# Trunk step on one core: squares of the output norm added on VectorE, one batch of token sums, and modulation steps in other places

## What is computed

```python
mod = silu(c) @ w_ada + b_ada              # nine rows of 1024: shift, scale, gate for three sublayers
x = x + 0.5 * gt1 * swiglu(rmsnorm(x) * (1 + sc1) + sh1)
proj = (rmsnorm(x) * (1 + scm) + shm) @ w_in
v = silu(layernorm(depthwise_causal_conv(a * sigmoid(g))) )     # 512 channels
p = pool_mix(u_pool)                                            # 512 channels
x = x + gtm * (concat[v, p] @ w_out)
x = x + 0.5 * gt2 * swiglu(rmsnorm(x) * (1 + sc2) + sh2)
y = rmsnorm(x)
```

## Time and profile before

| | |
|---|---|
| median of three runs | 1001.75 us |
| lowest, highest run | 1000.78, 1003.18 us |
| span of the profiled execution | 1000.3 us |
| mean granted TensorE clock in it | 0.995 of full speed |
| busy: TensorE, VectorE, ScalarE, GpSimd | 99%, 68%, 54%, 61% |
| TensorE idle while waiting, the longest after the start | 0.7, 0.6, 0.5 us |

### The profile page before, as it was taken

The page is one execution under the profiler, slowest core; times in us unless marked ns, Lnnn a source line. Parts: engine busy times, 40 slices in busy tenths (PEclk is TensorE's granted clock), DMA queues, the critical chain, the costliest instruction groups (busy, mean ns, idle before and its releaser), DMA issues.

```text
span 1000.3 us, 20132 instructions
## 1 busy us (share of the span) xinstructions
PE 986.4 (99%) x7589; PEld 948.4 (95%) x7589; DVE 676.6 (68%) x1391; ACT 538.4 (54%) x1000; POOL 610.6 (61%) x529
## 2 busy tenths in 40 slices
PE   9999999999999999999999999999999999999997
PEld 8899999999999998889977898999999999999996
DVE  3787766676666644469996447976666676666676
ACT  5756554566554542373264436665545665555664
POOL 3267666677676563346877143577666676766673
PEclk9999999999999999999999999999999999999998
DMA  9922322232224327745214622223222222223222
GB/s 360 376 82 90 123 85 86 86 117 94 85 86 168 128 85 291 271 160 204 85 34 169 254 91 79 85 85 118 93 86 86 102 111 85 86 90 122 85 86 95
DMA packets 22717, 127.52 MB, mean 127 GB/s; under 512 B 4192, under 2 KB 7392, under 8 KB 8032
## 3 DMA queue, kind: packets, MB, share of 16 engines
q1 hardware_dynamic: 19744, 105.28, 29.1%
q10 hardware_dynamic: 2880, 20.97, 5.5%
HBM read 123.06 MB, written 3.19 MB: 126 GB/s over the span
## 4 chain that ended last, share of the span: by engine, by line
PE 94%; POOL 2%; DVE 1%; ACT 1%; issue 1%; DMA 0%; DVEq 0%; POOLq 0%; ACTq 0%
PE tile_a L777 23%; PE tile_b L777 23%; PE ada_ps L777 18%; PE tile_a L610 8%; PE tile_b L610 7%; PE tile_a L750 3%; PE ada_ps L582 2%; PE tile_b L750 2%; PE tile_a L944 1%; PE tile_b L632 1%; POOL last_taps L2479 1%; PE ada_ps L956 1%; PE stat_ps L874 1%; PE tile_a L1019 1%; PE tile_a L661 1%
## 5 line engine op out<-in xcount | busy, mean ns | idle before, releaser
L2327 POOL TENSOR_TENSOR w_lo<-w_raw,w_hi 128x512 fp32r<-128x512 f32 (+1 forms) x177 | 226.0, 1283 | 96.1 <-ACT w_hi L1134 95.6
L2327 POOL TENSOR_TENSOR w_lo<-s_raw,w_hi 128x512 fp32r<-128x512 f32 (+1 forms) x118 | 152.3, 1292 | 74.5 <-ACT w_hi L1134 74.5
L1134 ACT ACTIVATE w_hi<-w_raw 128x512 fp32r<-128x512 f32 (+1 forms) x177 | 109.4, 619 | 66.8 <-PE ada_ps L777 53.4
L777 PE MATMUL tile_a<-x_hi,w_hi 128*128 128x288 f32 x400 | 118.7, 297 | 0.0
L777 PE MATMUL tile_b<-x_hi,w_hi 128*128 128x288 f32 x400 | 118.5, 296 | 0.0
L777 PE MATMUL tile_b<-x_lo,w_hi 128*128 128x288 f32 x400 | 118.2, 295 | 0.0
L777 PE MATMUL tile_a<-x_lo,w_hi 128*128 128x288 f32 x400 | 118.2, 295 | 0.0
L777 PE MATMUL tile_a<-x_hi,w_lo 128*128 128x288 f32 x400 | 117.8, 295 | 0.0
L777 PE MATMUL tile_b<-x_hi,w_lo 128*128 128x288 f32 x400 | 117.8, 294 | 0.0
L2283 POOL TENSOR_TENSOR w_lo<-w_raw,w_hi 128x2048 fp32r<-128x2048 f32 x13 | 59.7, 4591 | 80.6 <-ACT w_hi L1109 77.6
L777 PE MATMUL ada_ps<-x_hi,w_hi 128*128 128x288 f32 x320 | 94.9, 296 | 0.0
(11 more groups left out here) (349 smaller groups left out, 2977.7 us busy)
## 6 DMA issues: line engine op xcount, KB each, us to landing
w_raw<-w_units SPq DMA_DIRECT2D x78, 1024.0 KB, 4.8
ada_lo<-w_ada SPq DMA_DIRECT2D x16, 1024.0 KB, 8.0
ada_lo<-w_ada ACTq DMA_DIRECT2D x14, 1024.0 KB, 6.9
ada_hi<-w_ada ACTq DMA_DIRECT2D x6, 1024.0 KB, 6.2
x<-x_in SPq DMA_DIRECT2D x4, 576.0 KB, 5.9
y_out<-x SPq DMA_DIRECT2D x8, 288.0 KB, 2.5
conv_s<-conv_state SPq DMA_DIRECT2D x1, 480.0 KB, 10.8
conv_s_out<-conv_s SPq DMA_DIRECT2D x1, 480.0 KB, 4.3
```

The lines of the kernel that those rows point to most:

```text
L777: mm = pe.matmul(ps, slot(w, i)[:, P * k:P * (k + 1)], r, start=(first and n == 0 and k == 0), stop=(n == 2 and k == kc - 1), skip_group_c ...
L1134: nc.scalar.activation(slot(w_hi, i, wide(u)), source, ACT.Copy).then_inc(ready, 1)
L2327: return nc.gpsimd.tensor_tensor(slot(w_lo, i, n), raw, slot(w_hi, i, n).bitcast(F32), ALU.subtract)
```

## The change

The second add over chunks becomes a third: VectorE also adds the fourth chunk's squares, and TensorE makes one batch of token sums behind it (waiting for `ln_sq_added` >= 3). The last quarter of slot 6 is multiplied behind `out_chunk(3)` in place of between the batches, followed at once by the first quarter of slot 7; the transposition of slot 6 moves behind the quarters 7.1 and 7.2, its copy on ScalarE behind the four silu rounds, its bias add on VectorE behind the first two residuals of unit OUT. ScalarE's load of quarter 31 moves behind the silu rounds, its load of quarter 35 ahead of the last square, and its rounding of unit OUT+2 ahead of the copy of slot 7. GpSimd's list, its wait for `ln_sq_added` >= 2 and SyncE's list stay as they are.

```diff
@@ TensorE @@
             out_chunk(0)
             out_chunk(1)
-            pe.wait_ge(ln_sq_ready, CONV_CHUNKS)
-            token_sums(sums_ps, four[-1], True, False)
-            ada_products(6, 3)
-            pe.wait_ge(ln_sq_added, CONV_CHUNKS - 2)
-            token_sums(sums_ps, acc, False, True).then_inc(ln_var_mm, 1)
+            pe.wait_ge(ln_sq_added, CONV_CHUNKS - 1)
+            token_sums(sums_ps, acc, True, True).then_inc(ln_var_mm, 1)
             out_chunk(2)
             pe.wait_ge(ln_rstd_ready, 1)
             spread().then_inc(ln_r_ready, 1)
+            out_chunk(3)
+            ada_products(6, 3)
             ada_products(7, 0, 1)
-            out_chunk(3)
-            ada_turn(6)
             for k in range(GROUPS, KD):
                 out_chunk(k)
             ada_products(7, 1, 3)
+            ada_turn(6)
@@ ScalarE, squares(n, first_unit) @@
                     else:
+                        if n == 2:
+                            ada_load(ADA_QUARTERS * 9 - 1)
                         last_square(n)
                     if n == 1 and i < KD // 2 - 1:
                         ada_load(ADA_LATE + 2 * i + 4)
+                    if first_unit + i + 2 < UNITS and i < KD // 2 - 1:
+                        split_hi(first_unit + i + 2)
                     if n == 2 and i == 0:
                         ada_copy(7)
                         ada_load(ADA_QUARTERS * 8 + 2)
-                    if first_unit + i + 2 < UNITS and i < KD // 2 - 1:
-                        split_hi(first_unit + i + 2)
-
-            def ada_last_quarter(s):
-                ada_load(ADA_QUARTERS * s + ADA_QUARTERS - 1)
@@ ScalarE, behind the root @@
             load_table(ACT.Silu)
-            ada_copy(6)
...
                 vmix_round(c)
-                if c == 1:
-                    ada_load(ADA_QUARTERS * 8 - 1)
+            ada_load(ADA_QUARTERS * 8 - 1)
+            ada_copy(6)
             ada_load(ADA_QUARTERS * 8)
             ada_load(ADA_QUARTERS * 8 + 1)
 
             squares(2, OUT)
-            ada_last_quarter(8)
@@ VectorE, down_and_squares @@
+                    if n == 2 and i == 0:
+                        mod_evacuate(6)
                     if n == 2 and i == 2:
                         mod_evacuate(7)
@@ VectorE, layer norm @@
-            for c in range(1, CONV_CHUNKS - 1):
+            for c in range(1, CONV_CHUNKS):
                 dve.wait_ge(ln_sq_ready, c + 1)
                 if c == 1:
                     dve.wait_ge(pooled_lo_ready, GROUPS)
@@
-            mod_evacuate(6)
             down_and_squares(OUT, KD, GATE[1], 2)
```

## The result

The changed kernel is slower. Its median is 1007.66 us over six runs (1006.19 to 1013.19) beside 1002.05 us over six runs of the kernel before (1000.78 to 1004.18); the ratio of the times is 1.0063, with a 95% interval of 1.0050 to 1.0076. A later repetition gave 1.0048 (1.0034 to 1.0061), medians 1007.36 and 1001.96. One further execution of the kernel before, timed beside the experiments, took 1191 us at a mean granted clock of 0.751 and is left out of the ratios and medians here. The profiled execution took 1007.39 us, with a span of 1005.5; those of both kernels lie 1.9 us above their spans. The sign is as forecast, and so is the wait that brings it. The size and the clock behind that wait are not: the time lies 1.9 us above the upper end of the range.

What follows compares the result with a forecast made beforehand. TensorE, busy 99% of the span, was taken to bound the kernel. Terms -1.10 + 4.70 + 0 - 0.73 - 0.20 = +2.67 us, put onto the median 1001.75, gave 1004.4 us; range 998.0 to 1005.8.

Steps and rivals of the forecast that it cites:

- term 3: TensorE's clock at token sums, chunk 2 and spread: falls once and costs what it cost before, 0 us.
- The third add, +4.70: VectorE's third add of squares waits at SBUF for GpSimd's remainder of OUT+1, leaving TensorE idle: +4.70 us.
- the rival with a second stretch at 1.2 GHz: GpSimd first, TensorE's clock low for a second stretch after pause and sums: +1.3 us more, 1005.7 us; chance 0.16.
- the case without it: GpSimd first at SBUF, one stretch of TensorE at the low clock: the forecast 1004.4 us; chance 0.26.
- term 1: One batch of token sums less on TensorE in the norm, the whole of it counting: -1.10 us.
- Quarter 6.3 moved, 0: Quarter 6.3 moves behind chunk 3, slot 6's transposition behind 7.2; quarter 30's later load taken as harmless: 0 us.
- Copy, bias add and quarter 31, 0: ScalarE's copy of slot 6 and load of quarter 31, VectorE's bias add, all moved later without a wait: 0 us.
- The rounding of OUT+2, -0.73: ScalarE's rounding ahead of the copy of slot 7 removes TensorE's wait for the remainder of OUT+2: -0.73 us.
- Quarter 35, -0.20: ScalarE's load of quarter 35, issued ahead of the last square, removes TensorE's wait for it: -0.20 us.
- The quick cases (998.5 and 1000.05): VectorE takes SBUF before GpSimd: 998.5 us with the clock's gain (chance 0.32), 1000.05 without (0.12).
- the quick case: VectorE first at SBUF, short third add, clock stays up through chunk 2: -3.23 us, 998.5 us; chance 0.32.
- the last case: VectorE first, but the profile's clock fall was not in the runs of the median: 1000.05 us; chance 0.12.

Runs made afterwards that it cites:

- the moves alone: The changed kernel with the two adds and two batches of sums of the kernel before, back to back; ratio 0.9995 to the kernel before.

## Why the prediction was right or wrong

**One batch less, -1.10: right in count, undone by term 3.** The batch is gone; the one that is left took 2.15 us.

**The third add, +4.70: right.** The add was to be 5.1 us long and end 0.62 us behind GpSimd; it was 5.09 and 0.61. The idle time was 4.46 us, 4.62 with the start-up behind it. Quarter 6.3, moved away, would have filled 1.0 us of it. The lead of GpSimd, forecast from the gaps in the earlier trace rows as 0.03 or 0.04 us, was 0.025. I gave this order no more than 0.56, since the recorded starts might not be the order at SBUF. They were, at 0.025 us and, the other way about, at 0.045.

**The clock, 0: this step failed.** Term 3 puts the clock at nothing: "it falls once and costs what it cost". It fell during the pause and stayed at 1.2 GHz for twice as long, over the sums too: +1.05 in the sums, +0.12 in chunk 2, +0.13 in the spread, +1.30 in all. This is the rival with a second stretch at 1.2 GHz, at the price given there, +1.3, but its chance was 0.16 and the case without it 0.26. The mistake was to read the earlier trace rows as the cost of a fall, when the row shows only the chunk that it hit. With a pause in front, the sums were the first work under the low clock, and term 1 had priced them at 2.4 GHz. The Trainium skill ("TensorE: Matmul & The Clock Gate", HAM oscillation), as cited in the prediction, speaks of matmuls after a pause that start at the low clock; the trace agrees, with ten products at 0.50.

**Quarter 6.3 moved, 0: right, as far as loads go.** Quarter 30 was issued at 558.7 us and landed after 4.8 us in place of 9.0, in time for 7.2; unit OUT+3, queued behind it, took 6.9 us and was in time too.

**Copy, bias add and quarter 31, 0: right.** No wait has come from them.

**The rounding of OUT+2, -0.73: right, a little small.** Alone it gave -0.86. In the changed kernel it went ahead of the copy, then GpSimd's remainder, whose end at 576.13 lies 12.3 us ahead of the transposition of slot 7, where it lay 6.5 us ahead of it before:

```profile
569.55 1.90 ACT L1107 ACTIVATE w_hi<-w_raw 128x2048 fp32r<-128x2048 f32 x1
...
571.52 4.61 POOL L2279 TENSOR_TENSOR w_lo<-w_raw,w_hi 128x2048 fp32r<-128x2048 f32 x1 [22.76 <-ACT w_hi L1107]
```

**Quarter 35, -0.20: half right.** The wait is gone, but only 0.11 us of it reached the end.

**The sum.** Predicted +2.67; the trace shows 3.95 - 0.11 = +3.84, of which +1.30 is the clock, and the small rest is -0.13 in other terms. With the right clock term the prediction would have said 1005.7, just inside the range, and still 2 us too little. The second fault lies there: the sum was put onto a median of 1001.75 from three runs. The first profiled execution of before took 1002.2, and with +3.84 and the 1.37 us ahead of the stretch, which go with the early fall, it gives the 1007.4 of the profiled execution. The range took in the variation of the clock for the kernel before, in one rival, but not that the changed kernel might sit at its slow end.

**The rivals.** The quick cases (998.5 and 1000.05) need VectorE first. The changed kernel with the later wait of GpSimd and the one with VectorE's two waits swapped had it so, and took 1000.04 and 1000.06 us as medians. Their stretch lies 3.15 and 3.30 us below before's, for which the prediction worked out 0.35 - 1.10 - 1.55 - 0.73 = -3.03. So the sum of the quick case was good; the 998.5 us were not reached by the medians, which lie at the 1000.05 of the last case, in which the fall of the profile was not in the runs of the median. The mean clocks of the runs of before fit that, and no trace shows it.

**A version that beats both** came out: the changed kernel with either the later wait of GpSimd or the swapped waits, 0.9977 and 0.9974 of before. The first is the safer one, for its order does not hang on 0.045 us.

## What to carry to other kernels

Where VectorE and GpSimd both read SBUF with two operands and are released by the same event, hundredths of a microsecond can decide which of them waits for the whole instruction of the other: here it was the one that started second, each time. Put the order into a semaphore, so that the engine on the critical path goes first, or make the other's instructions short. Before work is taken away from in front of a wait on TensorE, ask what the clock will do in the pause that is left, and which matmuls come first behind it: the 1.10 us of the removed batch were paid again, 1.05 of them, by the remaining one at 1.2 GHz. And leave in front of such a wait what work there is: quarter 6.3 would have filled 1.0 us of it.

## What the runs showed that I had not expected

- The order of two waits on one VectorE instruction shifts its start from 0.104 to 0.035 us after its release, and here that turned +0.5% into -0.25%.
- The low clock came without any idle time in every profile of a kernel with two batches of sums (four: before twice, the rounding alone, the moves alone, where the batches stand back to back), and each time lasted 3.4 us. With one batch and no pause over 0.3 us it did not come (three profiles). Where TensorE paused for 2.3 to 4.5 us ahead of the one batch it lasted 6.8 us. It did so in every profile with such a pause that was left empty, five of them, three of the same kernel.
- A change in the middle of the kernel can look 1.6 us larger between medians than in the stretch that it touches. Falls of the clock that come in some executions and not in others make such differences: the one at 16 us is worth 1.3 us. Two profiles of one kernel, or the granted clock by stages, tell the two apart.
